# Query projection, cross attention and output projection of a decoder layer as one interleaved stage

## The reference

```python
x = x + concat(y_m, y_a) @ w_out
h = rms_norm(x, norm_cross)
q = rms_norm((h @ w_cq).reshape(B, T, 4, 256), cq_norm)
s = einsum('bthd,bmhd->bhtm', q, mem_k) * 256 ** -0.5
p = softmax(s)
o = einsum('bhtm,bmhd->bthd', p, mem_v).reshape(B, T, 1024)
x = x + o @ w_co
h = rms_norm(x, norm_ffn)
u = h @ w_up          # then a causal conv of width 3, GEGLU, down-projection
```

## Time and profile before

| | us |
|---|---|
| median of 3 runs | 1478.09 (1476.96 to 1481.18) |
| the profiled execution | 1482.92 |
| its span | 1481.2 |
| granted TensorE clock, mean | 0.846 of 2.4 GHz |
| PE busy | 1219.0 (82%) |
| DVE, ACT, POOL busy | 603.0, 478.7, 370.7 |

### The profile page before, as it was taken

One profiled execution on the slowest core, in us unless ns is written; L12 is line 12 of the kernel. 1 busy time (PEld: TensorE's weight loads), 2 busy tenths in 40 slices (PEclk: granted clock), 3 DMA queues, 4 the chain that ended last, 5 costly groups with the idle time before them and its releaser, 6 DMA issues.

```text
span 1481.2 us, 20549 instructions
## 1 busy us (share of the span) xinstructions
PE 1219.0 (82%) x7939; PEld 1037.5 (70%) x7939; DVE 603.0 (41%) x1166; ACT 478.7 (32%) x857; POOL 370.7 (25%) x194
## 2 busy tenths in 40 slices
PE   4768867668865874979787989788789999999998
PEld 3768756658852332659776953328689999999997
DVE  0234366785665455463322027622333334441000
ACT  4232232333231432013342221222345454553212
POOL 2112211112211121202254310002224344444342
PEclk9778787889975766559988975798989999999999
DMA  4212201122100123422235244241212332323332
GB/s 115 72 47 63 66 17 42 44 87 58 33 26 25 36 59 131 128 85 57 57 113 170 72 156 142 87 127 48 66 57 85 95 89 88 96 84 91 85 92 82
DMA packets 168330, 117.48 MB, mean 79 GB/s; under 512 B 7319, under 2 KB 158453, under 8 KB 167982
## 3 DMA queue, kind: packets, MB, share of 16 engines
q1 hardware_dynamic: 153632, 96.35, 22.0%
q0 software_dynamic: 2880, 10.49, 2.6%
q10 hardware_dynamic: 11760, 9.89, 2.1%
HBM read 107.62 MB, written 9.27 MB: 79 GB/s over the span
## 4 chain that ended last, share of the span: by engine, by line
PE 65%; DVE 17%; issue 9%; ACT 7%; POOL 1%; ACTq 1%; DMA 0%; DVEq 0%; POOLq 0%; PEldq 0%
PE PS L229 42%; PE PS L1447 3%; PE PS L1769 2%; PE PS L379 2%; PE PS L1198 1%; PE PS L1639 1%; PE PS L974 1%; ACT ikc L462 1%; PE PS L1709 1%; DVE xS L1721 1%; PE PS L1056 1%; PE PS L827 1%; POOL wlo L1436 1%; DVE tk L573 1%; DVE tiny L572 1%
## 5 line engine op out<-in xcount | busy, mean ns | idle before, releaser
L1436 POOL TENSOR_TENSOR wlo<-raw,whi 128x1024 fp32r<-128x1024 f32 x108 | 258.4, 2393 | 586.3 <-ACT whi L1421 586.3
L229 PE MATMUL PS<-ahi,whi 128*128 128x260 f32 x1584 | 336.8, 295 | 44.9 <-DVE alo L266 27.2
L229 PE MATMUL PS<-alo,whi 128*128 128x260 f32 x1584 | 328.8, 290 | 0.0
L229 PE MATMUL PS<-ahi,wlo 128*128 128x260 f32 x1584 | 327.9, 290 | 0.0
L229 PEld LDWEIGHTS PS<-ahi,whi 128*128 128x128 f32 x1584 | 255.3, 197 | 49.2 <-issue 24.2
L229 PEld LDWEIGHTS PS<-alo,whi 128*128 128x128 f32 x1584 | 254.7, 196 | 0.0
L229 PEld LDWEIGHTS PS<-ahi,wlo 128*128 128x128 f32 x1584 | 253.4, 195 | 0.0
L1421 ACT CAST whi<-raw 128x1024 fp32r<-128x1024 f32 x108 | 113.2, 1049 | 338.8 <-PE PS L229 338.6
L2224 POOL TENSOR_TENSOR wlo<-raw,whi 128x1024 fp32r<-128x1024 f32 (+1 forms) x31 | 73.0, 2358 | 314.4 <-ACT whi L2262 314.4
L1892 DVE SCALAR_TENSOR_TENSOR PS<-ub,cw,PS 128x512 f32<-128x512 f32 x44 | 33.2, 755 | 160.1 <-ACT PS L1870 160.1
L229 PE MATMUL PS<-gHi,whi 128*128 128x260 f32 x352 | 71.1, 283 | 0.0
(11 more groups left out here) (454 smaller groups left out, 1796.0 us busy)
## 6 DMA issues: line engine op xcount, KB each, us to landing
raw<-in_w_up SPq DMA_DIRECT2D x44, 512.0 KB, 3.7
raw<-in_w_in SPq DMA_DIRECT2D x30, 512.0 KB, 3.7
ckv<-in_cache_mem_k SPq DMA_DIRECT2D x8, 1024.0 KB, 6.1
ckv<-in_cache_mem_v SPq DMA_DIRECT2D x8, 1024.0 KB, 4.8
raw<-in_w_down SPq DMA_DIRECT2D x16, 448.0 KB, 3.7
raw<-in_w_out SPq DMA_DIRECT2D x8, 512.0 KB, 4.2
raw<-in_w_ck SPq DMA_DIRECT2D x8, 512.0 KB, 3.9
raw<-in_w_cv SPq DMA_DIRECT2D x8, 512.0 KB, 4.0
```

Source lines behind the costliest of these rows:

```text
L229: ins = nc.tensor.matmul(out[0:m, half, 0:HALF], w[:, s, k, 0:m], x[:, k0 + k, half * HALF:(half + 1) * HALF], start=(first and k == 0 and ...
L1436: nc.gpsimd.tensor_tensor(wlo[:, s], raw[:, s], whi[:, s].bitcast(F32), ALU.subtract).then_inc(split_full[s], 1)
```

## The change

The query projection, the cross attention and the output projection become one written-out order for each engine (`pe_fused`, `act_fused`, `vec_fused`, `sp_fused`, `pool_fused`). It has 16 slots: n = 0 to 7 after the tiles of `w_cq`, n = 8 to 15 after those of `w_co`.

- The 16 score blocks go in 8 pairs, p = 0 to 7, scored in slot 2 + p and turned in slot 3 + p. ACT takes the exponential straight from PSUM with `rq` as its scale (the factor 1/16 is in `mkT` now), and scales with the reciprocal sum itself (Identity); DVE only reduces, takes reciprocals and copies the turned blocks. Value products of heads 0 to 3 stand at n = 5, 7, after tile 1 and inside tile 3 of the output projection.
- The output projection is in two contraction halves: 8 tiles j, each 4 contraction steps x 256 output features (`pe_co`), over 512 columns in halves of 256. The first half (j < 4) needs heads 0 and 1 only. DVE adds twice to each x tile (`vec_co`).
- The sample key rows go one at a time through bank TA, in slots 6 to 14. For six of the eight sample rows (`POOL_KEYS`) ACT copies the row to `qb` and POOL multiplies (`pool_key`, between the splits of tiles 2 to 7); for the other two DVE multiplies. The product overwrites `ckv`; DVE sums.
- ACT's queue issues the first four cache loads as soon as the memory keys are made. SP issues the other twelve between the weight tiles.
- After the prompt's output projection: sample softmax; sample values, now with four outputs at partitions 0, 32, 64, 96 of one bank; then the samples' own output projection in plain float32 from `wS`, a second copy of `w_co` by rows (4 MB), their norm and split. The prompt's norm is computed by itself (512 columns), its sums of squares inside tiles 5 to 7 and behind them. `pe_hist` comes after the samples' projection, `vec_hist` after the norms.

The diff, cut:

```diff
+        SCORES = {2 + p: p for p in range(N_ATT // 2)}
+        TURNS = {3 + p: p for p in range(N_ATT // 2)}
+        SUMS = {2: 0, 4: 1, 6: 2, 7: 3}
+        POOL_KEYS = (0, 2, 3, 5, 6, 7)
+        TA_MID = {9: [(1, 0)], 10: [(1, 1)], 11: [(4, 0)], 12: [(5, 1)], 13: [(6, 1)], 14: [(7, 1)]}
+        TA_FIRST = {8: [(0, 0)], 9: [(2, 0)], 10: [(3, 0)], 11: [(4, 1)]}
+        TA_LAST = {6: ["q0"], 7: ["q1"], 8: [(0, 1)], 9: [(2, 1)], 10: [(3, 1)], 11: [(5, 0)], 12: [(6, 0)], 13: [(7, 0)]}
+        KEY_SUMS = {(9, 1): [0], (10, 0): [1], (10, 1): [2], (11, 1): [3, 4], (12, 1): [5], (13, 1): [6], (14, 1): [7]}
...
+        def pe_slot(pe, n):
+            pe_rows(pe, TA_FIRST, n)
+            if n in TURNS:
+                pe_cross_turn(pe, TURNS[n])
+            if n in SUMS:
+                pe_sums(pe, SUMS[n])
+            if n in SCORES:
+                pe_cross_score(pe, SCORES[n])
+            pe_rows(pe, TA_LAST, n)
...
+        def pe_co(pe, j):
+            s, base, part, jj = j % 2, BASE["co"], j // 4, j % 4
+            pe.wait_ge(split_full[s], base[s] + j // 2 + 1)
...
+                for k in range(4):
+                    if jj == 0 and o == 0:
+                        pe.wait_ge(y_lo, KT + 4 * part + k + 1)
+                    for t, (w, x) in enumerate(((hi, ahi), (hi, alo), (lo, ahi))):
+                        for half in range(2):
+                            m = nc.tensor.matmul(PJ[o][:, half, 0:2 * P], w[:, k, o * P:(o + 1) * P],
+                                                 x[:, 4 * part + k, half * 2 * P:(half + 1) * 2 * P],
+                                                 start=(k == 0 and t == 0), stop=(k == 3 and t == 2))
+                if o == 0:
+                    m.then_inc(co_half, 1)
+                    if j == 3:
+                        pe_cross_out(pe, 3, (XA, XB))
+                    pe_rows(pe, TA_MID, 8 + j)
+            m.then_inc(w_used[s], 1)
...
+            for j in range(KT):
+                pe_co(pe, j)
+                if j == 1:
+                    pe.wait_ge(co_free[0], 2)
+                    pe_cross_out(pe, 2, (PJ[0][:, 0, :], PJ[0][:, 1, :]))
+                if j == 5:
+                    pe.wait_ge(xa_read, H)
+                if j >= 5:
+                    pe_sumsq_prompt(pe, 2 * j - 10)
+                    pe_sumsq_prompt(pe, 2 * j - 9)
+                pe_slot(pe, 8 + j)
+            pe_sample_soft(pe)
+            pe_sumsq_prompt(pe, 6)
+            pe_sumsq_prompt(pe, 7)
+            pe_sample_turn(pe)
+            for b in range(B):
+                pe_sample_v(pe, b)
+            pe_sample_out(pe)
+            pe_sample_co(pe)
+            pe_hist(pe)
+            pe_sample_norm(pe)
+            pe.wait_ge(nlo_ready, 4 * KT)
+            pe.wait_ge(so_dve, SO_LO)
...
+            for i in range(2):
+                nc.scalar.activation(px[:, i], XA[:, i * NMEM:(i + 1) * NMEM], ACT.Exp, bias=xpair(1)[:, i:i + 1],
+                                     scale=rq[:, q0 + i, h:h + 1], accum_out=xpair(2)[:, i:i + 1]).then_inc(xa_exp, 1)
...
+        def vec_key_sum(dve, b):
+            if b in POOL_KEYS:
+                dve.wait_ge(kq_ready, POOL_KEYS.index(b) + 1)
...
+            for j in range(5):
+                weights(j)
+            cache(4)
+            weights(5)
+            cache(5)
+            cache(6)
+            weights(6)
+            sp.wait_ge(xa_scored, N_ATT // 2)
+            sp.wait_ge(qs_ready, 3)
+            rows(0)
+            rows(1)
+            cache(7)
+            cache(8)
+            weights(7)
+            sp.wait_ge(y_lo, 2 * KT)
+            rows(2)
+            rows(3)
+            cache(9)
+            up(0)
+            cache(10)
+            up(1)
+            for n in range(11, 2 * B):
+                cache(n)
...
+        def pool_key(pool, m):
+            b = POOL_KEYS[m]
+            pool.wait_ge(ckv_full[b % 4], 16 * (b // 4 + 1))
+            pool.wait_ge(ta_read, TA_USES.index((b, 1)) + 1)
+            k = ckv[b % 4]
+            nc.gpsimd.tensor_tensor(k[:], k[:], qb[:, m % 2].unsqueeze(1).to_broadcast([P, 2, D]), ALU.mult).then_inc(kq_ready, 1)
+
+        def pool_fused(pool):
+            for j, m in ((2, 0), (3, 1), (4, 2), (5, 3), (6, 4), (7, 5)):
+                pool_split_tile(pool, j)
+                pool_key(pool, m)
...
-            for half, bank in enumerate((TB, XB)):
+            for half in range(2):
                 for t in range(2):
-                    m = nc.tensor.matmul(bank[0:HB, :], xSm[:, b, t, :], ckv[b % 4][:, t, half * SEQ:(half + 1) * SEQ],
-                                         start=(b == 0 and t == 0), stop=(b == B - 1 and t == 1))
+                    r = HB * (2 * half + t)
+                    m = nc.tensor.matmul(TB[r:r + HB, :], xSm[:, b, t, :], ckv[b % 4][:, t, half * SEQ:(half + 1) * SEQ],
+                                         start=(b == 0), stop=(b == B - 1))
             m.then_inc(xs_used, 1)
...
+        def pe_sample_co(pe):
+            pe.wait_ge(so_dve, SO_OUT)
+            pe.wait_ge(ws_full, 16 * 4)
+            pe.wait_ge(ta_read, len(TA_USES))
             for k in range(KT):
+                for half, bank in enumerate((TA, TB)):
+                    m = nc.tensor.matmul(bank[0:B, :], oS[:, k, :], wS[k // 2][:, k % 2, half * SEQ:(half + 1) * SEQ],
+                                         start=(k == 0), stop=(k == KT - 1))
+            m.then_inc(so_pe, 1)
...
+        def pe_sample_norm(pe):
+            pe.wait_ge(so_act, SO_ROWS)
             for k in range(KT):
+                m = nc.tensor.transpose(TA[:, k * B:(k + 1) * B], co_row[:, k * P:(k + 1) * P], ident[0:B, 0:B])
+            m.then_inc(so_pe, 1)
+            pe.wait_ge(so_act, SO_SQUARES)
+            for k in range(KT):
+                m = nc.tensor.matmul(TB[:, 0:B], ones[:], sqS[:, k], start=(k == 0), stop=(k == KT - 1))
+            m.then_inc(so_pe, 1)
```

More of the change, by code:

```diff
@@ new lines, in pe_key_row, with pe_rows, pe_sumsq_prompt @@
+            m.then_inc(ta_full, 1)
+        def pe_rows(pe, table, n):
+            for use in table.get(n, []):
+                pe_key_row(pe, use)
+        def pe_slot(pe, n):
[7 more added lines that the diff above has]
+            pe_rows(pe, TA_LAST, n)
+        def pe_sumsq_prompt(pe, f):
+            pe.wait_ge(sq_ready, 3 * KT + f + 1)
+            nc.tensor.matmul(XA, ones[:], sq2[:, f % 2, 0:SEQ], start=(f == 0), stop=(f == KT - 1)).then_inc(sq_used, 1)
@@ new lines, in act_cross_out, with act_split_o, act_rows @@
+        def act_cross_out(act, h, src):
+            act.wait_ge(xa_done, h + 1)
+            S(nc.scalar.copy(oT[:, 2 * h:2 * h + 2, 0:SEQ], src), xa_read)
+        def act_split_o(act, k):
+            S(nc.scalar.copy(ahi[:, k, 0:SEQ], oT[:, k, 0:SEQ]), y_hi)
+        def act_rows(act, table, n):
+            for use in table.get(n, []):
+                if use in ("q0", "q1") or use[0] not in POOL_KEYS:
+                    continue
+                b, i = use
+                m = POOL_KEYS.index(b)
+                bank = ta_got(act, use)
+                if m == 0 and i == 0:
+                    act.wait_ge(mem_stored, 32)
+                if m >= 2:
+                    act.wait_ge(kq_ready, m - 1)
+                nc.scalar.copy(qb[:, m % 2, i * SEQ:(i + 1) * SEQ], bank).then_inc(ta_read, 1)
@@ new lines, in act_sample_co @@
+        def act_sample_co(act):
+            a = nc.scalar
+            act.wait_ge(so_pe, SO_CO)
+            for half, bank in enumerate((TA, TB)):
+                S(a.copy(co_row[:, half * SEQ:(half + 1) * SEQ], bank[0:B, :]))
+            act.sem_inc(so_act, 1)
+            act.wait_ge(so_dve, SO_ADDED)
+            a.activation(sqS[:], xT[:, :, SEQ:T], ACT.Square).then_inc(so_act, 1)
+            act.wait_ge(so_pe, SO_SUMS)
+            S(a.activation(rstdS[:], TB[:, 0:B], ACT.Ln, bias=epsc[:], scale=1.0 / D))
+            a.activation(rstdS[:], rstdS[:], ACT.Exp, scale=-0.5).then_inc(so_act, 1)
+            act.wait_ge(so_dve, SO_SCALED)
+            a.copy(ahi[:, :, SEQ:T], hS[:]).then_inc(so_act, 1)
```

635 lines of the change are left out of this document (379 added, 256 removed).

## The result

The changed kernel takes 1431.97 us (median of four runs, 1429.73 to 1433.72), the kernel before 1479.51 on the same chip. The ratio is 0.9672, with an interval of 0.9656 to 0.9688: faster by 48.5 us by the ratio. The forecast was 1423, in a range of 1412 to 1446, for a saving of 55.2. The profiled execution took 1431.99, of which 1430.3 are its span, 50.9 less than before.

What follows compares the result with a forecast made beforehand. The prediction took the slow stage as bound by waits between PE, DVE and ACT. 812.3 + 153.6 + 6.3 = 972.2, plus a 50.8 tail, put the up-projection at 1023.0, 55.2 less: 1478.1 - 55.2 = 1422.9 us, range 1412 to 1446.

Steps and rivals of the forecast that it cites:

- the slow stage: Kernel before, 876 to 946: a loop of PE, DVE and ACT, 7.35 us a turn, clock 0.55, no engine its bound.
- 153.6 of work: PE's work from the first query product to the end of the last output tile, at full clock: 153.6 us.
- the 4 for hand-overs: Allowance for PE waits up to the last output tile that the queue walk can't see: 4 us, bounds 0 and 15.
- the walk: Stepping through the engines' queues with the forecast prices: three PE waits of together 2.3 us before the last output tile ends.
- The estimate of twice the split: POOL's key product of 2048 elements priced as two splits of 1024: 4.8 us, bounds 2.4 and 9.6.
- The rival that POOL binds: POOL's key product takes 9.6 us, not 4.8; last key sum 8 us later: 1431, or 1459 at 14.4 each; chance 0.08.
- the 108 splits of even length: POOL's splits of 2.34 to 2.49 us in 108 cases, cited against POOL contending with DVE instructions with two SBUF inputs.
- Strips: Sample values: four products on four strips of output partitions run side by side, about 1.05 us a row warm.
- the series: Rival for the sample values: strips don't overlap, values take 30.7 us, 13.2 more in all, 1436.1; chance 0.20.
- The tail, term by term: After the last output tile: 8 + 15.2 + 3.0 + 16.5 + 2.8 + 5.3 = 50.8 us, up-projection at 1023.0.
- a sum: Part of the sample norm's term: eight transposes, a sum and six small steps, together 5.3 us, bounds 4 and 8.
- SP did not hold the weights back: Rival: on SP's queue weight tiles 6 and 7 and value loads come late, 10 to 20 us more, 1433 to 1443; chance 0.07.

Runs made afterwards that it cites:

- e6: Kernel before the change, with three extra float32 products of 512 columns in each of attention steps 0 to 7: 1476.82 us, ratio 0.9963 to that kernel.
- e4: Changed kernel with a second POOL product of the same size before each of the six POOL key products: 1444.60 us.
- e9: Changed kernel with two tiny DVE instructions, one with one SBUF input and one with two, ahead of each wait for a POOL key product: 1432.66 us, one run.
- e7: Changed kernel with the key product of sample row 7 on DVE instead of POOL: 1424.95 us.
- e11: Changed kernel with all eight key products on DVE and none on POOL: 1429.63 us.
- e1: Changed kernel with each sample value row's four products in two banks on the same 32 output partitions, as before the change: 1439.74 us.
- e2: Changed kernel without the loads of the last four sample value tiles; rows 4 to 7 read what the buffers hold: 1425.41 us.
- e10: Changed kernel with the first four cache loads issued from SP's queue between weight tiles instead of ACT's queue: 1430.14 us.
- e3: Changed kernel with the samples' output projection on four strips of output partitions: 1421.08 us.
- e8: Changed kernel with e3 and e7 together, sample values 4 to 6 loaded early, and the sample tail's steps reordered and shortened: 1401.04 us.

## Why the prediction was right, and where it was off

**The bound.** That the slow stage was a loop of waits and not an engine's limit holds: spread into the gaps of a dense stage, the same work leaves PE only 4.1 us of waits in 161. e6 lifts the clock to 0.87 and gains 5.5; by the estimate there, at most a third of the gain is the clock's. That PE's work would be the path up to the end of the output projection holds too, with 156.9 of 161.0 us busy.

**PE's work and its waits.** The sum was 153.6 of work and 6.3 of waits, 159.9; the window from 812 to 973 has 156.9 and 4.1, 161.0. The work was short by 3.3, and the 4 for hand-overs that the walk couldn't see was a guess that came out 2.2 too high: that the end of the last tile was met within 0.6 is in part luck. Key row products were priced as the value products, 0.89, and take 1.05, sixteen times: 2.6. That is half of the cold 2.08 of the earlier trace rows, and it was the nearer row. Further, one half tile ran cold, at 938.24:

```profile
938.24 4.56 PE PS L1699 x24
...
943.85 3.01 PE PS L1699 x24
```

It costs 1.5 more than the next one, behind the 1.4 of wait for DVE's product (L1915). Of the waits the walk gave one on DVE's product, and that came. It did not give the largest, 1.7 for the query rows (L1655). DVE's step ahead of it has two SBUF inputs and is held by POOL's split:

```profile
885.65 2.34 POOL L1445 TENSOR_TENSOR wlo<-raw,whi 128x1024 fp32r<-128x1024 f32 x1 [13.76 <-ACT whi L1430]
886.01 2.03 DVE L1892 TENSOR_TENSOR qs<-qT,gains 128x32 f32<-128x32 f32 x1
```

Where POOL is idle the same step takes 0.19. Both end at the same moment, within 0.05.

**POOL.** The estimate of twice the split, 4.8, was good:

```profile
L2054 POOL TENSOR_TENSOR ckv<-ckv,qb 128x2048 f32<-128x2048 f32 x6 | 27.5, 4584 | 27.0 <-ACT qb L1800 26.9
```

The rival that POOL binds would have had its price too low: with a doubled product the walk had the last key sum 8 later, in e4 it ends 15.8 later, and the kernel takes 11.8 more. The walk counted POOL's turns against PE's tiles. It took the last key for one among others, and it had no DVE step that POOL holds.

The contention was looked for at the wrong place. I took the 108 splits of even length as evidence that there is none; but they show only that POOL pays little. DVE pays: 1.84 for one element in e9, 2.03 and 1.22 (for 0.34, its length in the kernel before) in the changed kernel, 4.89 for 0.69 in e4. The kernel before had such rows too, beside the splits of line 2224, whose median is 2.37; L306 takes 0.42 else:

```profile
250.74 2.47 DVE L306 TENSOR_TENSOR rw<-rw,rope_m 128x256 f32<-128x256 f32 x1
```
```profile
250.31 2.61 POOL L2224 TENSOR_TENSOR wlo<-raw,whi 128x1024 fp32r<-128x1024 f32 x1 [8.21 <-ACT whi L2262]
```

In the Trainium skill, SBUF — State Buffer, SBUF: two separate sides, the two engines share a pair of ports under an exclusive lock: whichever starts first keeps it for its whole instruction, and a DVE instruction with two SBUF inputs is blocked meanwhile by a POOL instruction that reads SBUF. With that rule the traces agree both ways. Where POOL started first, DVE's step waits; where a DVE step with two SBUF inputs was running when POOL started, POOL's is longer: 2.61 for 2.37 above, and in e4 4.85 for 4.58 and 2.80 for 2.35.

L2086 is one that takes an input and a scalar from SBUF, and it was held as well, until 979.4, when POOL's split from 976.94 on had just ended. In e7 and e11 it takes 0.94 and ends just behind a split again. Whether the scalar or another property of the step is the reason, no run tells apart.

**Strips.** Right: 0.92 a row for the 1.05 taken, and e1 gives the series its 30.2. In the changed kernel's trace the records of the four strips start within 0.02 us of each other (983.46 to 983.48), each with its weight load. The Trainium skill's TensorEngine Tiling (Array Packing), Key Properties, is what this case's trace bears out; the strict reading of TensorE: Matmul & The Clock Gate, The mechanism, by which only another row group lets a weight load pass, is not, since here the row group was the same.

**The tail, term by term** (forecast, measured): end of the last output tile 972.2, 972.8; softmax 8, 9.0, of which 0.9 is L2086 held by POOL; values 15.2, 16.5; copy, transposes and additions 3.0, 3.2; projection 16.5, 16.7; history 2.8, 2.9; norm 5.3, 7.0. Together, unrounded, 5.0 late: 1023.0 became 1028.0. In the values, from the first product to the first reloaded row it is 6.6 for the 6.3 taken (the landing is 5.3 and not 4.8), and the last row ran cold at 1.98 for 1.1; the loads between them kept their distance. The norm was mis-sized by its products with ones: eight pairs of records with eight columns at about half clock take 3.59, where I had not priced them apart but let them go in "a sum". The loads bound the values and the prompt's norm (it ended at 993.1) was hidden, as forecast: its last cast ends at 992.4, 5.8 ahead of the values. In e2, without the loads, it holds the copy for 3.6.

**The queues.** SP did not hold the weights back, and the move from ACT's queue costs nothing (e10).

**What was forecast to show it.** Granted clock 0.95 or more from 815 to 970: 0.99. Value loads back to back at over 380 GB/s: the last four rows start at 988.33, 991.10, 993.66 and 996.18, on average 2.6 apart, which for 1 MiB are 401 GB/s. Idle time of PE inside the tiles over 15: 4.1.

**The 9 us between 1422.9 and 1432.0** are two things of like size. (The kernel before took 1.4 more here than the median that the forecast starts from, so the saving is short by 6.7 only.) For the profiled execution the forecast was 1427.7, and it took 1432.0: 5.0 of the terms above, and 0.3 because the stretch began 0.3 sooner than before and so was 5.3 longer than forecast, less 1.0 that was saved outside it. The other 4.8 is the step from that execution to the median: I gave the changed kernel the distance of the kernel before, whose profiled execution was longer than all its timed runs here; that of the changed kernel is at its median.

**What stays open.** Profiled executions of kernels that are alike up to there reach the first output product at 882.2 to 888.5. Most of the difference is there before 506: the same products run at the upper clock in one and at the lower in the other (0.80 in e1 from 400 to 450, 0.73 in the changed kernel). Why, no run shows. e3 and e7 gain some 4 us more by the ratio than in their profiles; in both the profiled execution was the longest of the four (1422.3 beside 1417.2 to 1422.2, 1428.7 beside 1423.1 to 1426.5). An earlier start of the others would explain it, but they have no profile.

## What to carry to other kernels

A stage of short steps on several engines that wait for each other is best spread into the gaps of a dense stage of TensorE: the waits are the larger part of the gain, and the clock came back with them (0.99 for 0.55). What is left behind such a merge is a serial tail, in which every step counts in full; ask of each product with few rows whether it can go to strips, of each load whether another buffer lets it start early, and of each copy what stands before it on its queue. When work goes to POOL, look for its price in DVE's instructions with two SBUF inputs and in what stands behind them on DVE's queue, more than in POOL's own rows.

## What the runs showed of the hardware

- Float32 products with 32 or 8 output rows on four strips of output partitions run side by side: 32 records of 512 columns in 3.69 us (32 rows, full clock), 6.23 (8 rows, cold to begin with) and 3.62 (8 rows, full clock), where one strip takes 13.9 for the 8 rows from a warm start (e1) and 16.7 from a cold one.
- A DVE instruction with two SBUF inputs that starts beside a running POOL product is not done before that product, even with one element: 1.84 us, 0.16 with POOL idle. A POOL instruction that starts beside such a DVE instruction is longer too, by 0.2 to 0.5 us in the rows above.
- The clock behind a short gap was the one ahead of it. Below, the windows between the last value row and the projection: the changed kernel's, behind four rows with waits of 2.97, 1.71, 0.62 and 0.59 us ahead of them, and e8's, behind eight rows without one. PE is idle for 2.0 us of the first and for 2.6 of the second, yet the projections begin at 0.50 and at 1.00. In the changed kernel the last three rows had run at the lower clock already (1.94 each), in e8 the last row ran at full clock (1.04). Waits of that size alone do not decide it: in e4 the last three rows had 1.81, 1.49 and 1.46 ahead of them and stayed at full clock (1.07 each), and the projection took 13.9. In e7 the last row took 1.65 and the projection 15.6, between the two.

```profile
998.20:1001.30 3.10, 1.12 (x4) 0.72 (x4) 1.11 (x5) 0.57 (x1) 0.00 (x0) 0.50 0.81 153
```
```profile
982.50:985.80 3.30, 0.66 (x4) 0.42 (x4) 1.71 (x6) 1.73 (x3) 0.00 (x0) 1.00 0.76 137
```
